# Value products of a 32-row sample tile in four column strips of TensorE: one change to a streaming encoder step on Trainium2

## What is computed

```python
def peer_ffn(h, wq, k1, k2, u, v):          # h: normalised rows
    q = (tb @ wq).reshape(P_BLOCK, P_HEADS, P_DKEY)
    ...                                      # the 16 best of 128 x 128 keys for each of 8 heads
    g = jax.nn.softmax(sc, axis=-1)
    pre = jnp.einsum('td,thkd->thk', tb, u[idx])
    act = (jax.nn.gelu(pre.astype(jnp.float32)) * g).astype(tb.dtype)
    return jnp.einsum('thk,thkd->td', act, v[idx])
```

```python
    x = x + jax.nn.sigmoid(rms_norm(x, lp['norm_ple_g']) @ lp['ple_w_gate']) * (p_i @ lp['ple_w_proj'])
```

## Time and profile before

| | us |
|---|---|
| median of 3 runs | 4756.58 (4755.93 to 4766.85) |
| span of the profiled execution, first to last instruction | 4754.3 |
| TensorE matmuls busy in it | 4255.9 (90%) |
| VectorE busy | 3116.5 (66%) |
| POOL busy | 1481.0 (31%) |
| ScalarE busy | 996.5 (21%) |
| first dot of the sample tile to the end | 4631.67 to 4754.3 |

### The profile page before, as it was taken

How to read it: one execution, slowest core, us unless ns; L and a number is a source line. 1 busy time by engine, 2 the same in 40 slices (tenths; PEclk the granted TensorE clock), 3 DMA queues, 4 the chain that set the end, 5 groups by cost and what they waited for, 6 DMA issues and landing times.

```text
span 4754.3 us, 50461 instructions
## 1 busy us (share of the span) xinstructions
PE 4255.9 (90%) x16837; PEld 2643.1 (56%) x16837; DVE 3116.5 (66%) x7138; ACT 996.5 (21%) x2580; POOL 1481.0 (31%) x1391
## 2 busy tenths in 40 slices
PE   8999999999898889888888999778988888888878
PEld 8999777888765675445443555323433433434332
DVE  3444113666377538887789777677777777777784
ACT  2222111234266301110111111111212111212212
POOL 1100002222111003444444444444444444444442
PEclk8999999999899999999999999999999999999999
DMA  2223222344323359999999999999999999999996
GB/s 93 69 89 124 88 91 75 123 129 129 110 77 109 113 180 369 396 413 410 417 405 409 403 416 405 420 420 403 409 409 419 385 402 416 397 416 408 383 413 259
DMA packets 310425, 1379.14 MB, mean 290 GB/s; under 512 B 37856, under 2 KB 112336, under 8 KB 175024
## 3 DMA queue, kind: packets, MB, share of 16 engines
q0 software_dynamic: 167728, 1166.48, 60.6%
q1 hardware_dynamic: 142464, 209.70, 12.8%
HBM read 1295.58 MB, written 80.49 MB: 289 GB/s over the span
## 4 chain that ended last, share of the span: by engine, by line
PE 31%; DMA 19%; DVE 10%; issue 4%; POOL 1%; ACT 0%; DVEq 0%; ACTq 0%; POOLq 0%
DMA peer_uv<-in_peer_uv_dram,peer_idx 19%; PE peer_acc L2740 19%; PE peer_fo L2675 4%; PE peer_fo L2688 2%; PE peer_fo L2576 2%; DVE peer_uv L2000 2%; PE peer_tb L2520 2%; DVE peer_diag L2030 1%; DVE peer_hot L1958 1%; DVE peer_hot L1961 1%; POOL peer_uv L1864 1%; DVE peer_sel L1964 1%; PE peer_fo L2594 0%; PE peer_acc L2624 0%; DVE peer_pos L1948 0%
## 5 line engine op out<-in xcount | busy, mean ns | idle before, releaser
L2740 PE MATMUL peer_acc<-peer_uv,peer_diag 128*128 128x512 f32 (+1 forms) x4000 | 1932.3, 622 | 303.5 <-DVE peer_diag L2030 296.3
L1864 POOL DMA_INDIRECT peer_uv<-in_peer_uv_dram,peer_idx x1056 | 1232.5, 1167 | 1704.5 <-PE peer_acc L2740 1577.2
L2000 DVE CUSTOM_DVE_ANT_0 peer_uv<-peer_uv,peer_h 128x1024 f32<-128x1024 f32 x1056 | 1290.7, 1222 | 639.9 <-DMA peer_uv<-in_peer_uv_dram,peer_idx 637.7
L2740 PEld LDWEIGHTS peer_acc<-peer_uv,peer_diag 128*128 128x128 f32 (+1 forms) x4000 | 742.3, 195 | 1285.5 <-issue 727.3
L2479 ACT ACTIVATE peer_ge<-peer_pre 128x1 f32<-128x1 f32 x1056 | 212.8, 203 | 2425.7 <-DVE peer_pre L2000 2425.1
L2675 PE MATMUL peer_fo<-peer_space 128*128 128x256 f32 (+2 forms) x1152 | 395.6, 475 | 42.0 <-DVE peer_space L2094 16.9
L99 PE MATMUL proj_bank<-proj_hTh,proj_wplead 128*128 128x352 f32 x1008 | 357.7, 355 | 1.8 <-DVE proj_wprest L91 1.8
L2030 DVE TENSOR_SCALAR peer_diag<-ident,peer_ge,peer_gw 128x128 f32<-128x128 f32 x968 | 332.2, 343 | 9.7 <-ACT peer_ge L2479 7.4
L2675 PEld LDWEIGHTS peer_fo<-peer_space 128*128 128x128 f32 x1152 | 221.7, 197 | 204.9 <-issue 157.8
L100 PE MATMUL proj_bank<-proj_hTr,proj_wplead 128*128 128x352 f32 x1008 | 328.8, 326 | 0.0
L101 PE MATMUL proj_bank<-proj_hTh,proj_wprest 128*128 128x352 f32 x1008 | 328.6, 326 | 0.0
(11 more groups left out here) (370 smaller groups left out, 5418.0 us busy)
## 6 DMA issues: line engine op xcount, KB each, us to landing
proj_wp<-in_w_in_dram POOLq DMA_DIRECT2D x13, 2048.0 KB, 9.8
peer_space<-in_w_ssm_o_dram SPq DMA_DIRECT2D x48, 512.0 KB, 7.6
peer_uv<-in_peer_uv_dram,peer_idx POOLq DMA_INDIRECT x1056, 12.1
proj_wp<-in_w_in_dram POOLq DMA_DIRECT2D x14, 1024.0 KB, 8.3
peer_space<-in_w_attn_o_dram SPq DMA_DIRECT2D x24, 512.0 KB, 7.9
peer_space<-in_w_out_dram SPq DMA_DIRECT2D x24, 512.0 KB, 7.8
scratch_xtok<-proj_shared SPq DMA_DIRECT2D x20, 512.0 KB, 3.2
scratch_chan<-proj_stg SPq DMA_DIRECT2D x48, 176.0 KB, 1.8
```

The costliest lines, as they stand in the source:

```text
L1864: pool.indirect_dma_start(uv[k][:], None, io["peer_uv"], bass.IndirectOffsetOnAxis(ap=idx[t % 2][:, col:col + 1], axis=0)).then_inc(uv_in[ ...
L2000: dve.tensor_tensor_reduce(uv[k][:, 0:D], uv[k][:, 0:D], h2[t % 2][:], 1.0, 0.0, ALU.mult, ALU.add, pre[g % 2][:, k:k + 1]).then_inc(u_don ...
L2740: x = pe.matmul(acc[0:r, h:h + HALF], diag[k][:, 0:r], uv[k][:, D + h:D + h + HALF], start=(it == 0 and k == 0), stop=False)
```

## The change

In the sample tile TensorE no longer takes slots one by one. After every fourth slot (k = 3 and k = 7) `four_products` makes the products of four slots together: it waits for the weights and the table rows of all four, and then writes slot q of the four into partitions 32q to 32q+31 of `acc`, that is, with the 32 columns of the array that belong to them. The four slots of one half of 512 columns are issued one behind the other, then those of the other half. `acc` then holds four partial sums on 128 partitions. The residual is added to the first of them. At the end ScalarE copies all of `acc` into `h2` (`parts_out`), TensorE multiplies that by `fold` into `acc[0:32]` (`parts_folded`), and the old copy follows.

```diff
+    QUADS = P // DEC
...
+        parts_out, parts_folded = s.sem("parts_out"), s.sem("parts_folded")
...
+                    if t == LAST:
+                        act.activation(h2[t % 2][:], acc[:], ACT.Copy).then_inc(parts_out, 1)
+                        act.wait_ge(parts_folded, 1)
                     act.activation((x2f if t == LAST else x2)[0:r, :], acc[0:r, :], ACT.Copy).then_inc(acc_out, 1)
...
+                def four_products(g, it, k0):
+
+                    pe.wait_ge(diag_done, products(g * SLOTS + k0 + QUADS - 1))
+                    for q in range(QUADS):
+                        pe.wait_ge(uv_in[k0 + q], g * 16 + 16)
+                    begins, ends_here = it == 0 and k0 == 0, it == TILE_ITS[LAST] - 1 and k0 + QUADS == SLOTS
+                    for h in range(0, D, HALF):
+                        for q in range(QUADS):
+                            x = pe.matmul(acc[q * DEC:(q + 1) * DEC, h:h + HALF], diag[k0 + q][:, 0:DEC], uv[k0 + q][:, D + h:D + h + HALF],
+                                          start=begins, stop=ends_here and q > 0)
+                            if h:
+                                x.then_inc(v_done, 1)
...
-                            if not aside(n):
+                            if t == LAST:
+                                if k % QUADS == QUADS - 1:
+                                    four_products(g, it, k + 1 - QUADS)
+                            elif not aside(n):
                                 pe.wait_ge(diag_done, products(n))
                                 pe.wait_ge(uv_in[k], g * 16 + 16)
...
                     x.then_inc(closed, 1)
+                pe.wait_ge(parts_out, 1)
+                for h in range(0, D, HALF):
+                    x = pe.matmul(acc[0:DEC, h:h + HALF], fold[:], h2[LAST % 2][:, h:h + HALF], start=True, stop=True)
+                x.then_inc(parts_folded, 1)
                 finish_last("turn")
```

## The result

| | before | changed |
|---|---|---|
| median over 14 runs each, us | 4758.41 (4755.8 to 4767.04) | 4767.21 (4760.47 to 4776.78) |
| ratio to before | | 1.0015, 95% interval 1.0008 to 1.0022 |
| span of the profiled execution | 4754.3 | 4760.7 |
| sample tile's first dot to its last | 83.8 | 88.7 |
| last dot to the end | 38.8 | 41.8 |

The changed kernel is slower by 8.8 us by the medians, 0.15% by the ratio. That is inside what I called no change, and beyond the 4 us of the forecast. The first dot of the sample tile stands at 4631.67 us before and at 4630.13 with the change, so the two parts of the last rows, together 122.6 and 130.5 us, are the better measure of what the change does: +7.9.

What follows compares the result with a forecast made beforehand. The sample tile was bound first by table transfers, then by TensorE. Six cycles of 67.4 us put group 7 at 4711.2; last dot, closing, fold and copies gave 4729.5 for 4725.57, +4 us: 4760.5, range 4751 to 4770.

Steps and rivals of the forecast that it cites:

- no change, slightly slower: Whole kernel: +4 us, 4760.5 us; chance 0.58 for this forecast, 0.71 for staying within 0.3%.
- fetches in bursts: Sample tile's ring of eight buffers: released four at a time, POOL's fetches come 10.4 to 12.1 us from burst to burst.
- low clock in the rests: TensorE between groups: long rests bring the 1.2 GHz level, so a group takes about 3.6 us in place of 1.9.
- fold on the path: After the sum closes: a new copy out of the accumulator, 1.05 us, and four fold records, 1.9 us.
- the 0.5 for the gate: Before group 5: 0.5 us allowed because 7.3 us of gate nearly fill the rest if group 4 runs long.
- Everything over X = 1.9 is lost, once in each of six cycles: Sample tile: with X a group's TensorE time, time over 1.9 us exceeds the transfers' 10.0 us cycle.
- X + 8.5: Cycle of four slots in us: group time X, 0.3 to refill start, 6.7 fetch to dot, 1.5 to group start.
- the fetch, taken as 6.7 us: From a fetch's start to its dot: 6.3 us from an empty queue, 7.1 with another close behind, 6.7 assumed.
- the 7 us: Sample tile: all groups at the high clock would give about 7 us less, down to the transfers' pace.
- transfers pace it: Sample tile: clock stays up, fetches return in 6.3 us, last dot about 4710.6; -5.5 us, 4751; chance 0.08.
- loads stick out: TensorE groups: exposed weight loads add 1.8 us in each of six cycles and group 8; 12.6 more, 4773; chance 0.17.
- no overlap: Strips run one after another: group time 6.9 + 0.2 us, about 9 starting low; +37, 4793; chance 0.14.

Runs made afterwards that it cites:

- d_one_strip: The changed kernel with all four slots of a group in the first 32 columns, without partial sums and fold: median 4774.72 us, ratio 1.0039.
- a_ungrouped: The changed kernel with strips and fold kept but no groups, each slot's product made and its buffer released alone: median 4756.55 us, ratio 0.999.
- c_filler: The changed kernel plus 30 filler matmuls adding zeros in TensorE's rests, meant to keep the clock high: median 4771.37 us, ratio 1.0023.
- g_pairs: The changed kernel with groups of two slots in place of four, strips in turn: median 4754.83 us, ratio 0.9989.
- the repeat: The changed kernel run again unaltered, beside later experiments on the same chip: median 4770.44 us, ratio 1.0022.
- h_residual_early: a_ungrouped with the residual added after slot 7 in place of after slot 31: median 4751.91 us, ratio 0.9976.
- f_hidden_fold: h_residual_early with partial sums of slots 0 to 23 folded at slot 24 and slots 24 to 31 in strip 0: median 4749.26 us, ratio 0.9977.

## Why the prediction was right, and where it was not

- **The forecast "no change, slightly slower" and its mechanism hold.** Backlog gone, fetches in bursts, low clock in the rests, fold on the path: all there. d_one_strip shows that the hold costs time to the last dot by itself, and a_ungrouped shows it to be avoidable.
- **Size.** By the profile +7.9, forecast +4; by the medians +8.8, and 6.7 over the forecast 4760.5, of which 1.8 are the base (4756.58 was the median of three runs, 4758.41 that of 14). From group 1's start to group 7's it was 70.3 us, forecast 67.4. Groups 3 and 4 were at the low clock (3.64 each; I had 1.9 and 3.0), 2.4 of the 2.9. For group 3 I had counted the embedding product as filling the rest; it ended 5.9 us before the group. The rest is in the wait outside the groups: the first fetch of a burst took 6.9 us on average in place of 6.7, and the 0.5 for the gate was not needed. The fold took 2.87, not 1.9, and the last gate 0.35 more in this profile. Group 8 and the residual together took 5.8 us where I had 6.2.
- **"Everything over X = 1.9 is lost, once in each of six cycles" is the weakest step.** X + 8.5 is right for the slow groups: the eight of both profiles of the changed kernel have X = 3.6 and cycles of 12.0 us on average. Behind the four fast ones the sum gives 10.4, and the cycles were 9.9 to 12.3, on average 11.4. So a fast group gave back 0.6 us and not 1.7. The term behind it is the fetch, taken as 6.7 us whatever is in the queue. In these two profiles it took 5.8 to 6.7 us where it left at most 2.8 us before the last dot of the burst before, and 6.3 to 8.65, on average 7.7, where it left 3.5 to 4.8 us before it. All four bursts behind fast groups are of the second kind. The row that I read as a queue run empty (4709.22 to 4715.48) was not one either: the slot ahead had its dot at 4711.82. As a price for the clock, the 7 us are not shown: c_filler got 1.3 to 2.6 us for 3.3 us of X.
- **Rival "transfers pace it"**: not in this kernel, but in a_ungrouped and g_pairs, with a last dot after 78.8 us as that rival had it (4710.6 less 4631.7).
- **Rival "loads stick out"**: fell, as shown above.
- **Rival "no overlap"**: fell. Its price was also wrong, 16 us by d_one_strip and not 37: missed was that in one strip the group's buffers come free one after another from its fifth matmul on. Its bounds for X do not follow from the sum either: with the other terms as they are, no gain is left at an average X of 2.0 us, not 2.4, and 0.3% is reached at 4.4, not 3.8.
- **Luck.** That the last gate could be left as it was held only for the first profile; in the repeat it is 2.8 us shorter, at the high clock, and nothing in the forecast says which it is.

## What to carry to other kernels

When work is batched, count how long the batch holds its buffers and compare with what the ring keeps in flight: here two of eight cost nothing and four cost 10 us to the last dot, twice what the faster product gave back (5 us in a_ungrouped). Column strips of TensorE need no batch: give consecutive small products different strips in turn, and they run together whenever a backlog has built up, and one by one otherwise. A new step at the very end counts in full, so move sums that are ready early (the residual, 1.8 us) off it first.

## What the runs showed that I had not expected

- Four float32 matmuls of 128 x 32 by 512 columns in four strips start within 0.02 us, with no cost against one (1.92 and 1.90 us for 16 and 4 records). In a_ungrouped a product in one strip ran beside the embedding product in another, into another tile (peer_sb), the two starting 0.02 us apart:

```profile
4669.82 0.62 PE L2667 MATMUL peer_acc<-peer_uv,peer_diag 128*32 128x512 f32 x1 [1.55 <-DVE peer_diag L2032]
4669.84 0.62 PE L2614 MATMUL peer_sb<-peer_space,peer_cs 128*32 128x512 f32 x1
```

- The first slot of a burst had its dot 3.9 to 4.6 us after the last of the burst before in five of six cases of the first profile, 3.0 to 4.4 us in the repeat, where 2.5 is the pace. That holds also where its fetch left 4.7 us ahead of that last dot (4692.51, 4697.21) and the DMA engines were busy in between: from 4697 to 4701 us they moved 369 to 418 GB/s at a share of 0.95 or more. After group 6 the step was 2.46 us with a fetch that left 3.8 us ahead, so it is no fixed cost. The likely cause is that a slot is there only when the slowest of 16 engines has its part, and that they part company in bursts. That is only argued; no run here separates it.
- The sample tile's first dot stood between 4630 and 4646 us in the ten profiles, in front of every edit. So single profiles are compared by stage. But the medians of a_ungrouped, g_pairs and h_residual_early fell short of their stage's gain by 6, 4 and 3 us, while f_hidden_fold's met it. The gains are taken against the one profile of the kernel before, whose last gate was 2.4 us longer than in these four; without the gate the four are 3.4, 1.4 and 0.9 us short and 2.3 us over. Whether the edits also move the time of the stages before (the programs differ in semaphores and length), or this is chance within intervals of 8 to 10 us, is open.
